# Two-block diffusion transformer on one core: order of the work at six stage boundaries

## What is computed

```python
h  = rmsnorm(x, norm_g) * (1 + scale) + shift         # latents; hc: the same for the context
# layer 0
y1 = diff_attend(q1, q2, k1, k2, v, lam)              # "a": 8 heads, two softmaxes per head
y1 = rmsnorm(y1 per head, a_sub_g) * (1 - lam_init)   # the head norms of "a"
y2 = attend(rope(q), rope(k), v, sink)                # "b": 8 query heads, 2 key heads, window
x  = x + gate * ((concat(y1, y2) * silu(ug)) @ w_o)   # and cx the same for the context
# layer 1
q, k = rope(rmsnorm(q, q_g)), rope(rmsnorm(k, k_g))   # "c": queries of the latents only
...                                                   # "d": low-rank attention, gate, w_o
x1 = rmsnorm(x, final_g)                              # end of the first block
# second block
h  = rmsnorm(x1, norm_g_2) * (1 + scale) + shift      # so two norms follow each other
```

## Time and profile before

| what | value |
|---|---|
| median of 3 runs | 3851.14 us (3845.43 to 3851.32) |
| the profiled execution's own time | 3854.37 us |
| its span in the trace | 3852.6 us |
| mean granted TensorE clock | 0.978 of full speed |
| busy: PE / DVE / ACT / POOL | 96% / 40% / 18% / 5% of the span |

### The profile page before, as it was taken

How to read it: one execution, slowest core, us unless ns; L and a number is a source line. 1 busy time by engine, 2 the same in 40 slices (tenths; PEclk the granted TensorE clock), 3 DMA queues, 4 the chain that set the end, 5 groups by cost and what they waited for, 6 DMA issues and landing times. The chain is left out here.

```text
span 3852.6 us, 68125 instructions
## 1 busy us (share of the span) xinstructions
PE 3680.0 (96%) x30170; PEld 2773.8 (72%) x30170; DVE 1552.4 (40%) x3025; ACT 680.1 (18%) x1614; POOL 189.5 (5%) x267
## 2 busy tenths in 40 slices
PE   5999999898998999999999999999999988999998
PEld 2489645455786676778747778566776777999998
DVE  2222343753334232212200441355555554655665
ACT  2100122420002122212100220122222221000001
POOL 0000000000000000000000000011222222000000
PEclk8999999999999999999999999999999997999999
DMA  9434222223442532365433334211111110444442
GB/s 378 172 143 167 100 106 88 88 88 153 175 175 78 206 131 74 145 253 207 153 131 131 119 123 143 88 47 37 47 45 38 47 35 24 155 176 174 170 170 110
DMA packets 73525, 490.16 MB, mean 127 GB/s; under 512 B 8448, under 2 KB 10496, under 8 KB 19472
## 3 DMA queue, kind: packets, MB, share of 16 engines
q1 hardware_dynamic: 70560, 462.45, 32.7%
q0 software_dynamic: 2672, 23.35, 1.6%
HBM read 481.57 MB, written 4.19 MB: 126 GB/s over the span
## 5 line engine op out<-in xcount | busy, mean ns | idle before, releaser
L1164 PE MATMUL ps<-h,w 128*128 128x256 f32 (+1 forms) x2816 | 927.4, 474 | 22.3 <-ACT h L1850 14.4
L1164 PEld LDWEIGHTS ps<-h,w 128*128 128x128 f32 x2816 | 521.0, 193 | 286.8 <-issue 236.8
L1280 PE MATMUL ps<-h,w 128*128 128x256 f32 (+1 forms) x1024 | 374.9, 500 | 1.4 <-issue 1.3
L1280 PEld LDWEIGHTS ps<-h,w 128*128 128x128 f32 x1024 | 180.6, 189 | 89.3 <-issue 69.5
L1427 PE MATMUL ps<-zone 64*64 64x64 f32 x4608 | 179.8, 220 | 7.5 <-issue 6.7
L2255 DVE TENSOR_TENSOR modc<-ps,bmod 128x4 f32<-128x4 f32 x72 | 11.4, 158 | 428.9 <-PE ps L1112 428.2
L1570 PE MATMUL ps<-h,zone 128*128 128x128 f32 (+1 forms) x1296 | 174.4, 288 | 0.0
L1427 PEld LDWEIGHTS ps<-zone 64*64 64x64 f32 x4608 | 162.9, 135 | 11.1 <-issue 9.3
L1158 PE MATMUL ps<-w,h 128*128 128x256 f32 x768 | 168.6, 380 | 0.0
L1570 PE MATMUL ps<-zone 128*128 128x128 f32 (+1 forms) x960 | 157.4, 313 | 9.8 <-DVE zone L2652 9.8
L1570 PEld LDWEIGHTS ps<-h,zone 128*128 128x128 f32 x1296 | 162.9, 193 | 4.9 <-issue 1.2
(11 more groups left out here) (452 smaller groups left out, 5156.1 us busy)
## 6 DMA issues: line engine op xcount, KB each, us to landing
w<-in_wm SPq DMA_DIRECT2D x128, 1024.0 KB, 6.7
w<-in_w SPq DMA_DIRECT2D x48, 1024.0 KB, 4.9
w<-in_we SPq DMA_DIRECT2D x34, 1024.0 KB, 5.0
w<-in_wi SPq DMA_DIRECT2D x34, 1024.0 KB, 4.9
w<-in_wrw SPq DMA_DIRECT2D x32, 1024.0 KB, 4.9
w<-in_wo SPq DMA_DIRECT2D x24, 1024.0 KB, 5.0
w<-in_wmg SPq DMA_DIRECT2D x24, 1024.0 KB, 6.1
w<-in_wbr SPq DMA_DIRECT2D x48, 512.0 KB, 4.5
```

Source lines behind the costliest of these rows:

```text
L1164: last = mm(pass_psum(s, q), rows[:, n * P:(n + 1) * P], src[k], start=(k == 0), stop=(k == s.kt - 1))
L1280: last = mm(ps[:, m, 0:T - NC * n], halves.rows(k)[:, m * P:(m + 1) * P], h[:, k, NC * n:T], start=(k == 0), stop=(k == KT - 1))
```

## The change

It reorders work at these boundaries, and alters one formula. The parts:

- Front: each of the four banks has its own signal, given in the last pair when the bank is complete, and ACT copies each before it turns to `lam`.
- Norms of "a": heads 0 to 6 are squared, summed, rooted and scaled inside the attention "a", summed at steps 17, 19, 21, 23, 25, 27 and 31, rooted and scaled one step later. Head 7 stays at steps 0 to 2 of "b".
- Rotations of `b_v` and `c_v` are spread over the matmuls; 16 matmuls follow the last rotation in both.
- Layer 0 to 1: one reciprocal and 16 `h` tiles of the latents, then the same for the context.
- Sums of `c_q` heads 0 to 2 come between its panels, the fourth after 8 matmuls of `c_k`, those of `c_k` after 8 matmuls of `c_v`.
- First to second block: the second root is taken of mean((xg)^2) + EPS (mean(x^2) + EPS), straight from both means; the first root and reciprocal follow after the `h` tiles.
- A one-column Sqrt is put on ACT early in `wo0` and early in `out`.

```diff
@@ front_pair (PE)
-                return last
+                    if p == 7:
+                        last.then_inc(s_front, 1)
...
-            front_pair(7).then_inc(s_front, 1)
+            front_pair(7)
@@ PE
+        NORM_AT = {0: 17, 1: 19, 2: 21, 3: 23, 4: 25, 5: 27, 6: 31}
+        norm_now = {at: hd for hd, at in NORM_AT.items()}
-            attend("a", beside("a"))
+            attend("a", beside("a"), lambda i: head_sum("a", norm_now[i]) if i in norm_now else None)
...
-                run(value, 32)
-                for r in ((0, 1), (2, 3, 4))[n]:
+                run(value, 16)
+                for r in ((0, 1), (3, 4))[n]:
                     rotate("b", r)
+                run(value, 16)
+                if n == 0:
+                    rotate("b", 2)
...
-            attend("b", beside("b"), lambda i: head_sum("a", i - 1) if 1 <= i <= 8 else None)
+            attend("b", beside("b"), lambda i: head_sum("a", 7) if i == 1 else None)
...
-            run(project("c_q", layer=1))
+            value = project("c_q", layer=1)
             for n in range(4):
-                head_sum("c1", n)
-            run(project("c_k"))
+                run(value, 32)
+                if n >= 1:
+                    head_sum("c1", n - 1)
+            run(value)
+            pe.wait_ge(s_hc, 2 * KT)
+            value = project("c_k")
+            run(value, 8)
+            head_sum("c1", 3)
+            run(value)
+            value = project("c_v")
+            run(value, 8)
             for n in range(2):
                 head_sum("c2", n)
-            value = project("c_v")
+            run(value, 8)
             pe.wait_ge(s_normed, norm_base["c2"][0])
-            for n in range(2):
-                run(value, 32)
-                if n == 1:
-                    pe.wait_ge(s_normed, norm_base["c2"][1] + 1)
-                for r in ((0, 1, 2), (3, 4))[n]:
-                    rotate("c", r)
+            for r in (0, 1):
+                rotate("c", r)
+            run(value, 16)
+            rotate("c", 2)
+            run(value, 16)
+            pe.wait_ge(s_normed, norm_base["c2"][1] + 1)
+            for r in (3, 4):
+                rotate("c", r)
+            run(value)
@@ ACT
+            for c in range(4):
+                act.wait_ge(s_front, c + 1)
+                f(pass_dst(segs["a_qk"], c // 2, c % 2), ps[:, c, :], ACT.Copy).then_inc(s_fev, 1)
             act.wait_ge(s_lam, 2)
             f(lam[:, 2:4], lam[:, 0:2], ACT.Exp).then_inc(s_lam, 1)
-            act.wait_ge(s_front, 1)
-            for c in range(4):
-                f(pass_dst(segs["a_qk"], c // 2, c % 2), ps[:, c, :], ACT.Copy).then_inc(s_fev, 1)
...
+            def early_heads(i):
+                if i in norm_now:
+                    act.wait_ge(s_oe, base["a"] + 4 * norm_now[i] + 4)
+                    square("a", norm_now[i])
+                if i - 1 in norm_now:
+                    root("a", norm_now[i - 1])
...
+            f(warm[:, :], sel[:, 0:1], ACT.Sqrt)
...
-            for t in range(KT):
-                for who in (1, 0):
+            for who in (0, 1):
+                for t in range(KT):
                     shift(1, t, who, e)
...
+            value = take("c_q")
+            for n in range(4):
+                next(value)
+                next(value)
                 if n >= 1:
-                    root("c1", n - 1)
-            root("c1", 3)
+                    query_square(n - 1)
+            run(value)
+            query_square(3)
+            for n in range(4):
+                root("c1", n)
...
-            layer_root(4, 0, NL)
             layer_root(5, 0, NL, lr2)
+            layer_root(5, 0, NL)
@@ DVE
+            def early_heads(i):
+                if i in norm_now:
+                    head_mean("a", norm_now[i])
+                if i - 1 in norm_now:
+                    head_scale("a", norm_now[i - 1])
...
-            v_.reciprocal(lr[:, 0:NL], lr[:, 0:NL])
-            link(v_.reciprocal(lr[:, NL:T], lr[:, NL:T]))
-            for t in range(KT):
-                h_tile(1, t, 1, lr[:, 0:NL])
-                h_tile(1, t, 0, lr[:, NL:T])
+            for who, cols in ((0, slice(NL, T)), (1, slice(0, NL))):
+                link(v_.reciprocal(lr[:, cols], lr[:, cols]))
+                for t in range(KT):
+                    h_tile(1, t, who, lr[:, cols])
...
             layer_mean(3, ps[:, 4, 0:NL], NL)
+            link(v_.tensor_scalar(lr2[:, 0:NL], ps[:, 4, NL:T], 1.0 / D, None, ALU.mult))
+            v_.scalar_tensor_tensor(lr2[:, 0:NL], lr[:, 0:NL], EPS, lr2[:, 0:NL], ALU.mult, ALU.add).then_inc(s_lms, 1)
             dve.wait_ge(s_lrt, 4)
-            link(v_.reciprocal(lr[:, 0:NL], lr[:, 0:NL]))
-            link(v_.scalar_tensor_tensor(lr2[:, 0:NL], ps[:, 4, NL:T], 1.0 / D, lr[:, 0:NL], ALU.mult, ALU.mult))
-            link(v_.tensor_tensor(lr2[:, 0:NL], lr2[:, 0:NL], lr[:, 0:NL], ALU.mult))
-            v_.tensor_scalar(lr2[:, 0:NL], lr2[:, 0:NL], EPS, None, ALU.add).then_inc(s_lms, 1)
-            dve.wait_ge(s_lrt, 5)
             link(v_.reciprocal(lr2[:, 0:NL], lr2[:, 0:NL]))
-            link(v_.tensor_tensor(lr2[:, 0:NL], lr2[:, 0:NL], lr[:, 0:NL], ALU.mult))
             for t in range(KT):
                 v_.scalar_tensor_tensor(h[:, t, NC:T], xl[:, t, :], gain2[:, t:t + 1], lr2[:, 0:NL], ALU.mult, ALU.mult)\
                     .then_inc(s_hs, 1)
+            dve.wait_ge(s_lrt, 5)
+            link(v_.reciprocal(lr[:, 0:NL], lr[:, 0:NL]))
```

More of the change, by code:

```diff
@@ L291, in build @@
         sel = sb("sel", [P, 2])
+        warm = sb("warm", [P, 1])
         cond = sb("cond", [P, KT, 4])
@@ L2094, in _ @@
                     copy_after(name, j)
-            attend("a", beside("a", take))
+            def early_heads(i):
[4 more added lines that the diff above has]
+                    root("a", norm_now[i - 1])
+            attend("a", beside("a", take), early_heads)
             run(take("b_v"))
@@ L2099, in head_part @@
             def head_part(i):
-                if i < 8:
-                    square("a", i)
-                if 2 <= i <= 9:
-                    root("a", i - 2)
+                if i == 0:
+                    square("a", 7)
+                if i == 2:
+                    root("a", 7)
             attend("b", beside("b", gate_tanh), head_part)
@@ L2125, in _, with query_square @@
             layer_root(2, 0, 512)
-            for t in range(KT):
-                for who in (1, 0):
+            for who in (0, 1):
+                for t in range(KT):
                     shift(1, t, who, e)
                     e += 1
-            run(take("c_q"))
-            for n in range(4):
+            def query_square(n):
                 b, q = pass_no["c_q", n, 1] % 2, pass_no["c_q", n, 1]
@@ L2232, in _ @@
                 keep_first(by_panel["out", j])
+                if j == 0:
+                    f(warm[:, :], sel[:, 0:1], ACT.Sqrt)
                 if j >= 1:
@@ L2762, in _ @@
                     rope_apply("a", 2 * (n - 5) + 1)
-            attend("a", beside("a", adds))
-            value = adds("b_v")
-            for n in range(2):
-                next(value)
-                for r in ((0, 1), (2, 3, 4))[n]:
-                    rope_apply("b", r)
-            run(value)
+            def early_heads(i):
[3 more added lines that the diff above has]
+                    head_scale("a", norm_now[i - 1])
+            attend("a", beside("a", adds), early_heads)
+            for r in (0, 1):
+                rope_apply("b", r)
+            run(adds("b_v"))
+            for r in (2, 3, 4):
+                rope_apply("b", r)
             dve.wait_ge(s_bias, 16)
             def head_part(i):
-                if 1 <= i <= 8:
-                    head_mean("a", i - 1)
-                if 2 <= i <= 9:
-                    head_scale("a", i - 2)
+                if i == 1:
+                    head_mean("a", 7)
+                if i == 2:
+                    head_scale("a", 7)
             attend("b", beside("b", lambda part, js: gate(part, y512, js, norm_base["a"][0])), head_part)
@@ L2827, in _ @@
                 head_scale("c2", n)
-            value = adds("c_v")
-            for n in range(2):
-                next(value)
-                for r in ((0, 1, 2), (3, 4))[n]:
-                    rope_apply("c", r)
-            run(value)
+            for r in (0, 1):
+                rope_apply("c", r)
+            run(adds("c_v"))
+            for r in (2, 3, 4):
+                rope_apply("c", r)
             def low_rank(i):
```

## The result

| what | before | after |
|---|---|---|
| median of 4 runs each, us | 3848.39 (3845.43 to 3851.32) | 3815.39 (3814.43 to 3817.71) |
| ratio, with its 95% interval | | 0.9913 (0.9901 to 0.9926) |
| the profiled execution's own time, us | 3854.37 | 3814.43 |
| its span, us | 3852.6 | 3812.6 |
| mean granted TensorE clock | 0.978 | 0.980 |

The direction was right. The forecast gain was 27.6; the medians show 33.0 (28 to 38 by the interval). Of the 8.1, 2.75 come from the base: the forecast took 3851.14 for the kernel before, the median of three runs, and with a fourth run it is 3848.39.

What follows compares the result with a forecast made beforehand. PE, busy for 96% of the span, was taken as the bound, so reordering could only win back its idle or slow time. Terms summed to 27.6 us off the 3851.14 median: 3823.5 us, range 3815 to 3840.

Steps and rivals of the forecast that it cites:

- the price of a removed wait: At the stage boundaries: each removed PE wait gains the length of its bracket, less 0.1 us for a hand-over.
- the price in "a": Attention "a": head norms moved there make PE wait, mostly for scores; loss 1.4 us, bounds 0 and 8.0.
- front: Front: PE's wait of 1.22 us for two bank copies shrinks to a hand-over of 0.1; gain 1.1 us.
- rotations of `b_v`: Between attentions "a" and "b": PE's waits of 1.24 and 2.87 us go, less a hand-over; gain 4.0 us.
- norms out of "b": Attention "b": waits of 6.5 us from head norms go, except 0.3 for the one head left; gain 6.2 us.
- layer 0 to 1: Start of layer 1: PE starts 2.2 us earlier and waits less for tiles in `c_q`; gain 4.3 us.
- "c", its three sum waits counted: Before attention "c": rotation waits go, gain 4.5 us; three waiting sums in `c_q` cost 1.0 us.
- lower clock: Behind removed waits at "b", in "b" and at "c": slow PE stretches go too; 2.4, 1.5 and 3.0 us.
- R2: Rival: head norms cost attention "a" the 8.0 us they cost "b", not 1.4; gain 21.0, 3830.1 us; chance 0.08.
- R4: Rival, slower: nothing of a head norm is hidden at the scores of "a"; 11.0 us slower, 3862.1; chance 0.05.
- R3: Rival: a drain of 1.38 us follows each ScalarE table load in "a"; gain 19.3, 3831.8 us; chance 0.03.
- R1: Rival: slow-clock stretches stay or fall elsewhere, so 6.9 us do not come back; gain 20.7, 3830.4 us; chance 0.10.

## Why the prediction came out 5 us short

The step that failed is the price of a removed wait: the terms of the front, of `b_v`, of "b" and of "c" enter it at the length of its bracket, less 0.1 for a hand-over. Forecast at 13.4 together (the price in "a" taken off), they measure 17.0 when each edit stands alone. With the other two terms 20.7 were forecast, and 25.2 were measured. The second step that failed is the sum of the clock, which allowed for slow stretches that go and for none that come. Point by point, clock-free, in us. The last row but one of the table sets the sum of the parts beside the whole change.

| term | forecast | measured alone |
|---|---|---|
| front | 1.1 | 1.5 |
| rotations of `b_v` | 4.0 | 4.5 |
| norms out of "b", less their price in "a" | 6.2 - 1.4 = 4.8 | 8.1 - 1.7 = 6.4 |
| layer 0 to 1 | 4.3 | 5.1 |
| "c", its three sum waits counted | 3.5 | 4.6 |
| second root | 3.0 | 3.15 |
| sum of the parts | 20.7 | 25.2 (the whole change: 25.4) |
| lower clock | 6.9 | 5.7 between the first profiles, 2.9 between the second ones (19.8 to 16.9) |

**What held.** The places and kinds of every wait. `c_q` waits 4.38 (forecast 4.1 to 4.2), the second block 4.69 (4.8), three waits of 1.11, none at the start of "b" and "c". In "a", where the trace of before showed nothing and I budgeted DVE's steps, 1.36 of waits came for 1.4, though not where I put them: 0.26 at step 18 (0.4), 0.24 at step 24 (0.7), none at step 19 (0.3), and 0.86 at two sums that waited for ACT's square, which I had not listed. The 0.7 was too much in part because the copy-out was put at 0.5, where it takes 0.29:

```profile
578.40 0.29 DVE L2379 COPY y<-ps 128x128 f32<-128x128 f32 x1 [2.02 <-PE ps L1259]
```

R2 and R4 are refuted for this placement; R3 as well: an exponential starts 0.01 us after its load in the new place too, and no wait of the scores inside "a" is above 0.26. The timeline of ACT at step 18 after:

```profile
549.61 1.28 ACT L1904 ACT_TABLE_LOAD   x1 [2.54 <-PE ps L1244]
550.90 0.69 ACT L1904 ACTIVATE zone<-ps,st 128x512 f32<-128x512 f32 x1
```

The Trainium skill (ScalarE: Activation LUTs, What ACT_TABLE_LOAD costs) counts a drain of some 1380 ns with each load, which would have to show there, and does not; nor does it show ahead of a load, which starts 0.02 us after the activation before it at 1204.70 in the kernel without the one-column Sqrt.

**What failed, by size.** *"PE waits 1.22 us ...", and so on: each term was the bracket of a wait.* PE's idle time fell by 19.8. What was left out is the 5.6 us by which its busy time at the upper clock fell as well. One source is shown above: behind a wait the next group is not overlapped (0.16) and longer (0.08). "b" lost five waits and 8.1 us for 6.5 idle; the start of "b" two and 4.5 for 4.1; the front one and 1.5 for 1.2. I had even deducted 0.1 for hand-overs, with the wrong sign. The other source is in the layer 0 to 1 term.

*"With 6.0 us at the lower clock, as behind the wait of "c" ... 10.2 us, the second 7.2"*: the first two passes were forecast at 17.4 and took 15.94. I borrowed the 3.0 us of clock from another boundary, where this one lost 2.0 before and 1.9 after; clock-free the two passes go from 17.5 to the 14.4 of my forecast, 3.1, and with the start of 2.2 the term would have been 5.3, against 5.1 measured alone. The term for the waiting of each matmul, 0.77 to 0.44, was right; the records show that waiting as busy time. The 5.3 and 5.1 are clock-free and so leave out what the clock hides behind the tiles in before; with the clock in, it is 4.5 for 4.3 when the edit stands alone. In "c" 0.2 of the 1.1 short belongs to the wait fewer; for the rest I have no reading.

**What failed, by mechanism.** *"The slow stretch ... goes with the wait that precedes it."* By place this held. Over the 14 traces here, the wait of 2.87 before "b" has its slow stretch in all seven traces that have the wait (1.7 to 2.6 us lost, forecast 2.4), the wait of 2.63 in "b" in all eight (1.7, forecast 1.5), and the wait of 3.37 before "c" in five of seven (3.1, 3.1, 2.9, 1.6 and 1.4, forecast 3.0); where the wait is gone, the stretch is gone. R1 (all 6.9 stay) did not come: the clock term is 19.8 to 20.7 in the five traces in which all three waits stay and 14.3 to 17.6 in the eight others (the kernel with three reciprocals left out). What failed is the silence on the rest. A wait need not bring a slow stretch, as the two traces with nothing before "c" show; the trace of before had a case, the wait of 2.58 at the first scores of "a", which the earlier trace rows and the words "2.6 us and more" passed over. And the new front puts a stretch behind that very wait, 1.6 us, which no term allowed for. That, and the scatter behind "d" (1.7 and 3.0 in the two profiles of before, 2.4 and 4.3 in those of after), is how 6.9 became 5.7 or 2.9.

**The range.** Its low end took "the upper bounds of the two norm boundaries (3.0 and 2.0) and the scatter of runs". All six terms were too small, most of them for one common reason, and one-sided errors add: 4.5. The low end should have allowed for that, say 3810. (The waits listed at the head of the prediction sum to 33.0 and not 32; nothing was worked out from that sum.)

Left open: what brings a slow stretch (not tried by itself), what more than the brackets "c" gave back, and why the recurrence varies between 774.5 and 783.0 us over the kernels here, 5.6 of it between two executions of one. Up to the recurrence the first two profiles differ by 31.2 us and the second two by 28.7; the medians say 33.0, with an interval of 28 to 38. The 2 to 4 us between are found in no stretch that the change touches and may be chance.

## What to carry to other kernels

Price a removed wait at its bracket plus the overlap that the next group gets back, here 0.2 to 0.3 us each, and look for waits shorter than the trace's resolution where one engine follows another tile by tile. Work that delays PE in one stage can be moved to another if the time of the busiest helper engine is budgeted step by step; then test the edge by tripling that work, since a placement that costs next to nothing may also have next to nothing left. Compare stage by stage and clock-free: six parts, each worth 1.5 to 6.4 us of 3850, could be told apart in single profiles where medians with intervals of 7 to 15 us could not.

## What the runs showed of the hardware that was not expected

The lower clock costs these kernels 14 to 21 us of PE's time up to the recurrence (20.05 before, 14.3 and 16.9 after, 20.5 with the front edit alone). Where it falls differs between two executions of one file (3.1 and 1.4 us lost behind the same wait), and with an edit far upstream: the wait of 2.58 at the first scores of "a" has a slow stretch behind it in seven of seven traces with the new front, and in none of seven with the old. A stretch of unchanged code that waits for weights takes 300.3 to 302.6 us over the kernels here, clock-free. And a table load does not wait for the operand of the activation that needs it: without the warming operation it still ran 4.6 us ahead of the root.
